# Regrouping a unit's sixteen products in an FFN up projection: by width, in place of alternating widths

## The chip, the cores and the metric

The kernel runs on one core of one Trainium2 chip. The metric is the device time of one execution in microseconds; the time before is the median of three runs.

## The reference, cut to what matters

One layer of a hybrid encoder trunk on 256 tokens of width 2048, in float32:

```python
h = rms_norm(x, attn_norm);  p = h @ w_in          # 2048 -> 5376 columns, then attention and a gated recurrence
x = x + concat(attn_out, hg_out) @ w_out           # 2048 -> 2048
h = rms_norm(x, ffn_norm)
u = h @ w_up                                       # 2048 -> 11264 columns, the projection that is changed
u = sum(conv_w[j] * up[:, j:j + S] for j in range(3)) + conv_b
a, b = split(u, 2)
x = x + (silu(a) * b) @ w_down                     # 5632 -> 2048
```

## The kernel before, in words

Precision is kept by splitting. Every float32 weight tile is split into a high part `w_hi` (ScalarE's copy to fp32r, `make_hi`, line 445) and a remainder `w_lo` (VectorE's subtraction, `make_lo`, line 781), and the activations lie in `hs` as high and low halves side by side: `hs[:, tile, 0:256]` is the high part of 256 tokens, `hs[:, tile, 256:512]` the low part. A product of two split numbers is three products: high x high, high x low and low x high.

Weights come in units of 128x1024 float32 (512 KB), through a ring of four slots (`RING = 4`) with one buffer each of `raw`, `w_hi` and `w_lo` per slot. For a slot the order is: SyncE's queue loads `raw` once VectorE has split what was in it before (semaphore `units_split`, lines 325 to 329); ScalarE makes `w_hi` once the load has landed and TensorE has used the unit before it in this slot (`loaded`, `units_used`, lines 442 to 445); VectorE makes `w_lo` (lines 779 to 782) and counts `units_split`; TensorE waits for that count, multiplies, and counts `units_used` with the unit's last product.

The up projection (`unit_channels`, line 1254) has 44 groups of 256 output channels, four units to a group, so 176 units. A unit is four tiles of the contraction (k) times two tiles of 128 output channels (b), and each of these eight has its own accumulator bank. Per k and b it issues two products, each with its own weight load:

- line 1262: weights `w_hi`, moving `hs` in its full 512 columns, which is high x high and high x low at once, into all 512 columns of the bank;
- line 1263: weights `w_lo`, moving the 256 columns of the high half, added into the first 256 columns of the same bank.

So before the change the widths go 512, 256, 512, 256 and so on, 16 products to a unit. When a group is done VectorE adds the two halves of each bank (`evacuate`, line 784) and runs two taps of the convolution (`taps`, line 1170); ScalarE runs the third tap and the silu. Two pairs of banks alternate between groups (`pair_of`, line 285). Lines 1544 to 1560 issue the stage: two groups written out, then a loop of 21 with two groups in each turn.

Two other helpers show what TensorE does with one width alone. `unit_w_in` (line 1267) issues 24 products of 256 columns, lines 1276, 1278 and 1279. `unit_tokens` (line 1283, output and down projections, lines 1292 to 1294) and `unit_i_and_g` (line 1419, lines 1428 to 1430) issue 12 products of 512 columns each. In all of them each product has a 128x128 weight load of its own, as here.

Of the kernel before, what the change touches and what calls it, by code (L numbers as in the profile page):

```python
# [38 lines left out]
P = 128  # L39
D_MODEL, SEQ, CHUNK = 2048, 256, 64  # L40
# [7 lines left out]
RING = 4  # L48
FREE = 1
BANK_PAIRS = 2  # L50
GC = 256
# [37 lines left out]
def hybrid_layer(nc, x, attn_norm, w_in, q_norm, k_norm, sinks, lb_logits, hg_norm, w_out,  # L89
                 ffn_norm, w_up, conv_w, conv_b, w_down, out):  # L90
    ctx = ExitStack()
    with ctx:
        def sb(name, shape, dt=F32):
            return ctx.enter_context(nc.sbuf_tensor(name, shape, dt))
# [13 lines left out]
        hs = sb("hs", [P, KT, 2 * SEQ], F32R)  # L108
        raw = sb("raw", [P, RING, 1024])
        w_hi = sb("w_hi", [P, RING, 1024], F32R)  # L110
        w_lo = sb("w_lo", [P, RING, 1024], F32R)
# [173 lines left out]
        def pair_of(group):  # L285

            b = 2 * ((group + 1) % BANK_PAIRS)
            return bank[b], bank[b + 1]
# [937 lines left out]
        def _(pe):  # L1226
            def transpose(dst, src, n=P):
                return pe.transpose(dst, src, ident[0:n, 0:n])  # L1228
# [25 lines left out]
            def unit_channels(quad, i, group):  # L1254

                pe.wait_ge(units_split, quad * RING + i + 1 + RING)
                banks = pair_of(group)
                for k in range(4):
                    for b in range(2):
                        c = slice(k * GC + b * P, k * GC + (b + 1) * P)  # L1260
                        x_k = hs[:, 4 * i + k, :]
                        pe.matmul(banks[b][:, :], w_hi[:, i, c], x_k, start=(i == 0 and k == 0), stop=False)  # L1262
                        last = pe.matmul(banks[b][:, 0:SEQ], w_lo[:, i, c], x_k[:, 0:SEQ], start=False,  # L1263
                                         stop=(i == RING - 1 and k == 3))
                last.then_inc(units_used, 1)

            def unit_w_in(quad, i, dst):
# [48 lines left out]
            for i in range(RING):  # L1316
                pe.wait_ge(h_lo, 2 * i + 2)
                unit_w_in(0, i, bank[0])
                if i == 2:
# [4 lines left out]
                    for c in range(1 + CONV):  # L1324
                        at = N_SMALL + c * N_CONV
                        last = transpose(bank[3][:, at:at + N_CONV], rows[0:N_CONV, 1 + c, :], N_CONV)
# [218 lines left out]
            for i in range(RING):  # L1545
                pe.wait_ge(h_lo, (CHUNKS + i + 1) * TT)
                unit_channels(Q_UP, i, G_UP)
                if i == 1:
                    second_norm(OUT_GROUPS - 1)
            pe.wait_ge(groups_evacuated, G_UP + 2)  # L1550
            for i in range(RING):
                unit_channels(Q_UP + 1, i, G_UP + 1)
                if i == 0:

                    spread_rms(1)
            with pe.Fori(1, UP_GROUPS) as g:
                for ab in range(2):
                    pe.wait_ge(groups_evacuated, g * 2 + ab + G_UP + 1)
                    for i in range(RING):
                        unit_channels(g * 2 + ab + Q_UP, i, G_UP + ab)  # L1560
# [37 lines left out]
```

## Time and profile before

| what | before |
|---|---|
| median of 3 runs | 1123.79 us (1123.77 to 1123.81) |
| the profiled execution, its own time | 1132.9 us |
| its span, first to last instruction | 1131.1 us |
| TensorE (matmul) busy | 1122.8 us, 99% |
| TensorE weight load busy | 972.9 us, 86% |
| VectorE busy | 786.8 us, 70% |
| ScalarE busy | 588.8 us, 52% |
| DMA | 204.26 MB, mean 181 GB/s |
| granted TensorE clock over the span | 0.999 |

All durations below come from the one profiled execution, which is 9.1 us longer than the median of the runs without a profile. In the timeline a row is one instruction: its start, its duration, the engine, the line of the kernel, what it writes and reads. Matmuls are pipelined: one starts while the one before it is still draining, so the duration in a row is longer than the step from one start to the next, and the pace of TensorE is read from the starts. The up projection's first product starts at 388.76 us and its last at 887.77 us of the span.

### The profile page before, as it was taken

How to read it: one execution, taken by the hardware profiler on the slowest of the kernel's cores; microseconds unless marked ns; L12 is line 12 of the kernel's file. 1: busy time of each engine (PE TensorE's matmuls, PEld its weight loads, DVE VectorE, ACT ScalarE, POOL GpSimd, SP SyncE). 2: the span in 40 equal slices, each digit the busy share in tenths (PEclk: the TensorE clock that was granted, in tenths of full speed). 3: DMA queues.
4: the chain of work that ended last, by engine and by line, in shares of the span. 5: the costliest groups of instructions: out<-in, count | busy, mean ns of one | idle time of the engine just before them, and what ended most of it. 6: DMA issues, size and time to landing. Idle time of an engine off the chain costs nothing.

```text
span 1131.1 us, 18722 instructions
## 1 busy us (share of the span) xinstructions
PE 1122.8 (99%) x6593; PEld 972.9 (86%) x6593; DVE 786.8 (70%) x1178; ACT 588.8 (52%) x863; POOL 11.1 (1%) x43
## 2 busy tenths in 40 slices
PE   9999999999999999999999999999999999999998
PEld 8989898989888888888888888888888888888887
DVE  5788968778755577777777777777777745454443
ACT  7678565657444565555555555555555533433332
POOL 3000000000000000000000000000000000000000
PEclk9999999999999999999999999999999999999999
DMA  8544555554556556555656565556665566666562
GB/s 264 154 148 120 179 154 166 164 172 150 171 184 188 186 175 193 184 186 185 186 184 187 184 187 185 186 184 187 185 186 183 188 192 195 210 194 211 191 214 80
DMA packets 172514, 204.26 MB, mean 181 GB/s; under 512 B 6949, under 2 KB 140470, under 8 KB 172214
## 3 DMA queue, kind: packets, MB, share of 16 engines
q1 hardware_dynamic: 171302, 201.55, 57.5%
q10 hardware_dynamic: 1168, 2.11, 0.5%
q8 instruction: 28, 0.46, 0.2%
q14 instruction: 16, 0.13, 0.0%
HBM read 201.54 MB, written 2.10 MB: 180 GB/s over the span
## 4 chain that ended last, share of the span: by engine, by line
PE 89%; DVE 7%; ACT 3%; issue 0%; ACTq 0%; DVEq 0%
PE bank L1262 29%; PE bank L1263 15%; PE bank L1292 10%; PE bank L1294 10%; PE bank L1293 10%; PE bank L1276 3%; PE bank L1278 3%; PE bank L1279 3%; DVE w_lo L781 2%; ACT w_hi L445 1%; PE bank L1228 1%; PE bank L1428 1%; DVE E L997 1%; DVE E L976 1%; PE bank L1429 1%; PE bank L1430 1%
## 5 line engine op out<-in xcount | busy, mean ns | idle before, releaser
L781 DVE TENSOR_TENSOR w_lo<-raw,w_hi 128x1024 fp32r<-128x1024 f32 x380 | 463.1, 1223 | 285.8 <-ACT w_hi L445 285.1
L445 ACT CAST w_hi<-raw 128x1024 fp32r<-128x1024 f32 x380 | 398.3, 1052 | 455.2 <-PE bank L1263 197.7
L1262 PE MATMUL bank<-hs,w_hi 128*128 128x512 f32 x1408 | 497.9, 399 | 0.2 <-DVE hs L801 0.2
L1263 PE MATMUL bank<-hs,w_lo 128*128 128x256 f32 x1408 | 395.4, 281 | 0.0
L1262 PEld LDWEIGHTS bank<-hs,w_hi 128*128 128x128 f32 x1408 | 264.6, 188 | 66.5 <-DVE hs L801 0.5
L1263 PEld LDWEIGHTS bank<-hs,w_lo 128*128 128x128 f32 x1408 | 265.9, 189 | 0.1
L1293 PE MATMUL bank<-w_lo,gated 128*128 128x512 f32 x352 | 136.9, 389 | 0.0
L1292 PE MATMUL bank<-w_hi,gated 128*128 128x512 f32 x352 | 136.9, 389 | 0.0
L1294 PE MATMUL bank<-w_hi,gated 128*128 128x512 f32 x352 | 136.9, 389 | 0.0
L1276 PE MATMUL bank<-hs,w_hi 128*128 128x256 f32 x416 | 120.5, 290 | 0.6 <-DVE w_lo L781 0.6
L1278 PE MATMUL bank<-hs,w_hi 128*128 128x256 f32 x416 | 117.6, 283 | 0.0
L1279 PE MATMUL bank<-hs,w_lo 128*128 128x256 f32 x416 | 117.6, 283 | 0.0
L1276 PEld LDWEIGHTS bank<-hs,w_hi 128*128 128x128 f32 x416 | 79.6, 191 | 3.0 <-issue 2.6
L1278 PEld LDWEIGHTS bank<-hs,w_hi 128*128 128x128 f32 x416 | 79.7, 192 | 0.4 <-issue 0.2
L1279 PEld LDWEIGHTS bank<-hs,w_lo 128*128 128x128 f32 x416 | 79.6, 191 | 0.0
L1294 PEld LDWEIGHTS bank<-w_hi,gated 128*128 128x128 f32 x352 | 66.1, 188 | 13.8
L1293 PEld LDWEIGHTS bank<-w_lo,gated 128*128 128x128 f32 x352 | 66.1, 188 | 13.7
L1292 PEld LDWEIGHTS bank<-w_hi,gated 128*128 128x128 f32 x352 | 66.1, 188 | 13.6
L1179 DVE SCALAR_TENSOR_TENSOR C<-U,cols,C 128x256 f32<-128x256 f32 x176 | 73.4, 480 | 0.0
L727 ACT ACTIVATE C<-U,cols 128x256 f32<-128x256 f32 x88 | 48.2, 595 | 25.3 <-DVE U L792 25.3
L1428 PE MATMUL bank<-w_hi,hs 128*128 128x512 f32 x128 | 50.8, 397 | 0.0
L1292 PE MATMUL bank<-w_hi,mix 128*128 128x512 f32 x128 | 50.3, 393 | 0.0
(189 smaller groups left out, 957.4 us busy)
## 6 DMA issues: line engine op xcount, KB each, us to landing
raw<-in_w_ffn_up_dram SPq DMA_DIRECT2D x176, 512.0 KB, 3.5
raw<-in_w_ffn_down_dram SPq DMA_DIRECT2D x88, 512.0 KB, 4.4
raw<-in_w_in_dram SPq DMA_DIRECT2D x52, 512.0 KB, 3.8
raw<-in_w_in_dram SPq DMA_DIRECT2D x64, 256.0 KB, 2.9
raw<-in_w_out_dram SPq DMA_DIRECT2D x32, 512.0 KB, 3.9
xt<-in_x_dram SPq DMA_DIRECT2D x2, 1024.0 KB, 6.0
out_dram<-xt ACTq DMA_DIRECT2D x3, 512.0 KB, 6.7
out_dram<-xt ACTq DMA_DIRECT2D x2, 256.0 KB, 2.5
```

Of the source, the lines that this page charges most:

```text
L445: act.copy(w_hi[:, i, :], raw[:, i, :]).then_inc(units_hi, 1)
L781: dve.tensor_tensor(w_lo[:, i, :], raw[:, i, :], w_hi[:, i, :].bitcast(F32), ALU.subtract)\
L1179: dve.scalar_tensor_tensor(C[:, ab, c, :], U[:, c, tap:tap + SEQ], cols[:, bass.ds(col, 1)], C[:, ab, c, :], ALU.mult, ALU.add).then_inc(a ...
L1262: pe.matmul(banks[b][:, :], w_hi[:, i, c], x_k, start=(i == 0 and k == 0), stop=False)
L1263: last = pe.matmul(banks[b][:, 0:SEQ], w_lo[:, i, c], x_k[:, 0:SEQ], start=False, stop=(i == RING - 1 and k == 3))
L1276: pe.matmul(o, w_hi[:, i, c], x_hi, start=(i == 0 and k == 0 and b == 0), stop=False, skip_group_check=True)
L1278: pe.matmul(o, w_hi[:, i, c], x_lo, start=False, stop=False, skip_group_check=True)
L1279: last = pe.matmul(o, w_lo[:, i, c], x_hi, start=False, stop=(i == RING - 1 and k == 3), skip_group_check=True)
L1292: pe.matmul(banks[t][:, :], x_hi, hi, start=(k0 + k == 0), stop=False)
L1293: pe.matmul(banks[t][:, :], x_hi, lo, start=False, stop=False)
L1294: last = pe.matmul(banks[t][:, :], x_lo, hi, start=False, stop=(k0 + k == k_all - 1))
L1428: pe.matmul(o, x_hi, hi, start=(u == 0 and k == 0), stop=False)
```

## The change

Within `unit_channels` the one loop over k and b becomes two. The first issues the eight 512-column products with `w_hi`, the second the eight 256-column products with `w_lo`. The same sixteen products with the same operands go into the same banks. Consecutive products now go to the two banks in turn, where before two in a row went to each. The wait at the start, the start flag on the first product of each bank, and the count `units_used` on the last product of the unit stay.

```diff
                 for k in range(4):
                     for b in range(2):
                         c = slice(k * GC + b * P, k * GC + (b + 1) * P)
-                        x_k = hs[:, 4 * i + k, :]
-                        pe.matmul(banks[b][:, :], w_hi[:, i, c], x_k, start=(i == 0 and k == 0), stop=False)
-                        last = pe.matmul(banks[b][:, 0:SEQ], w_lo[:, i, c], x_k[:, 0:SEQ], start=False,
-                                         stop=(i == RING - 1 and k == 3))
+                        pe.matmul(banks[b][:, :], w_hi[:, i, c], hs[:, 4 * i + k, :],
+                                  start=(i == 0 and k == 0), stop=False)
+                for k in range(4):
+                    for b in range(2):
+                        c = slice(k * GC + b * P, k * GC + (b + 1) * P)
+                        last = pe.matmul(banks[b][:, 0:SEQ], w_lo[:, i, c], hs[:, 4 * i + k, 0:SEQ],
+                                         start=False, stop=(i == RING - 1 and k == 3))
                 last.then_inc(units_used, 1)
```

## Rows read from the trace of the kernel before

**Rows 1.** The page: span, busy time of the engines, granted clock.

```profile
span 1131.1 us, 18722 instructions
...
PE 1122.8 (99%) x6593; PEld 972.9 (86%) x6593; DVE 786.8 (70%) x1178; ACT 588.8 (52%) x863; POOL 11.1 (1%) x43
...
PEclk9999999999999999999999999999999999999999
```

**Rows 2.** Windows of 500:600 (up) and 888:1000 (down); busy by engine, clock, DMA.

```profile
500.00:600.00 100.00, 100.00 (x568) 86.67 (x567) 76.84 (x105) 51.53 (x62) 0.00 (x0) 1.00 0.60 187
...
888.00:1000.00 112.00, 112.00 (x496) 92.75 (x495) 55.93 (x52) 44.92 (x45) 0.00 (x0) 1.00 0.63 198
```

**Rows 3.** Waits in 410:880, up projection: total us, times, longest us.

```profile
ACT w_hi L445 <- PE bank L1263: 193.0, 140, 1.8
DVE w_lo L781 <- ACT w_hi L445: 100.8, 83, 1.6
```

**Rows 4.** The page's costliest groups: busy us, mean ns, idle before.

```profile
L1262 PE MATMUL bank<-hs,w_hi 128*128 128x512 f32 x1408 | 497.9, 399 | 0.2 <-DVE hs L801 0.2
L1263 PE MATMUL bank<-hs,w_lo 128*128 128x256 f32 x1408 | 395.4, 281 | 0.0
```

**Rows 5.** Timeline of PE, up projection, widths in turn: start us, us, instruction.

```profile
599.91 0.40 PE L1262 MATMUL bank<-hs,w_hi 128*128 128x512 f32 x1
600.15 0.28 PE L1263 MATMUL bank<-hs,w_lo 128*128 128x256 f32 x1
...
605.21 0.40 PE L1262 MATMUL bank<-hs,w_hi 128*128 128x512 f32 x1
```

**Rows 6.** Timeline of PE, a long run of 512-column products.

```profile
121.87 0.39 PE L1428 MATMUL bank<-w_hi,hs 128*128 128x512 f32 x1
...
132.75 0.39 PE L1428 MATMUL bank<-w_hi,hs 128*128 128x512 f32 x1
```

**Rows 7.** Timeline of PE, 256-column products right after a 512-column run.

```profile
143.40 0.28 PE L1276 MATMUL bank<-hs,w_hi 128*128 128x256 f32 x1
...
143.75 0.28 PE L1276 MATMUL bank<-hs,w_hi 128*128 128x256 f32 x1
143.87 0.28 PE L1278 MATMUL bank<-hs,w_hi 128*128 128x256 f32 x1
...
146.15 0.28 PE L1279 MATMUL bank<-hs,w_lo 128*128 128x256 f32 x1
```

**Rows 8.** Timeline of PE, first and sixth 512-column product after 256-column ones, twice.

```profile
117.09 0.40 PE L1428 MATMUL bank<-w_hi,hs 128*128 128x512 f32 x1
...
118.25 0.39 PE L1430 MATMUL bank<-w_hi,hs 128*128 128x512 f32 x1
...
887.88 0.40 PE L1292 MATMUL bank<-w_hi,gated 128*128 128x512 f32 x1
...
889.04 0.39 PE L1294 MATMUL bank<-w_hi,gated 128*128 128x512 f32 x1
```

**Rows 9.** Timeline of PE, the first three products of the up projection.

```profile
388.76 0.39 PE L1262 MATMUL bank<-hs,w_hi 128*128 128x512 f32 x1
388.99 0.28 PE L1263 MATMUL bank<-hs,w_lo 128*128 128x256 f32 x1
389.10 0.40 PE L1262 MATMUL bank<-hs,w_hi 128*128 128x512 f32 x1
```

**Rows 10.** Timeline of PE, up projection between two interruptions, widths in turn.

```profile
399.24 0.40 PE L1262 MATMUL bank<-hs,w_hi 128*128 128x512 f32 x1
...
403.40 0.40 PE L1262 MATMUL bank<-hs,w_hi 128*128 128x512 f32 x1
```

**Rows 11.** Timeline of ACT and DVE: the split of one unit.

```profile
608.24 1.05 ACT L445 CAST w_hi<-raw 128x1024 fp32r<-128x1024 f32 x1 [1.78 <-PE bank L1263]
...
609.56 1.22 DVE L781 TENSOR_TENSOR w_lo<-raw,w_hi 128x1024 fp32r<-128x1024 f32 x1
```

**Rows 12.** The page's DMA issues: count, KB each, us from issue to landing.

```profile
raw<-in_w_ffn_up_dram SPq DMA_DIRECT2D x176, 512.0 KB, 3.5
```

## The prediction

> **What bounds the kernel now.** I read the page first. TensorE is busy for 1122.8 of 1131.1 us and its granted clock is at the full level in all 40 slices [rows 1]. That says that TensorE carries the span and that no clock is to be won, but not that it runs at its best pace, because a pipelined matmul counts as busy while it drains. The page's groups show how far this goes: the 1408 products of line 1262 and the 1408 of line 1263 sum to 497.9 + 395.4 = 893 us of duration [rows 4], in a stage that lasts 499 us (388.76 to 887.77). So these durations can't be added, and the pace must be taken from starts.
>
> Next the windows by stage. In the up projection TensorE is busy for all of the 100 us, VectorE for 76.84, ScalarE for 51.53, and the DMA engines move 187 GB/s [rows 2]. The waits of the stage have no row for TensorE at all: ScalarE waits for TensorE (193.0 us in 140 waits) and VectorE for ScalarE (100.8 us) [rows 3]. Everyone waits, directly or through another, for TensorE to free a slot. The stage takes as long as TensorE needs for its stream of products, so what a reordering of the stream is worth is a question of start-to-start steps alone.
>
> So I read the timeline for three kinds of stretch. **Widths in turn**, as now: line 1262 starts at 599.91 and, 15 pairs later, at 605.21 [rows 5], so a pair takes 5.30 / 15 = 353.3 ns. **512 columns alone**: 48 steps from 121.87 to 132.75 [rows 6], 226.7 ns each. **256 columns alone**: 19 steps from 143.87 to 146.15 [rows 7], 120.0 ns each. Apart, the two widths would cost 226.7 + 120.0 = 346.7 ns; in turn they cost 6.7 ns more. That surplus, in 1408 pairs, is what the regrouping can reach.
>
> **The change, part by part.**
>
> *The runs.* A unit now takes 8 x 353.3 = 2826.7 ns. Two runs of eight at their own steady steps would take 8 x 226.7 + 8 x 120.0 = 2773.3 ns, 53.3 ns less.
>
> *The changes of width that remain*, one each way per unit where there were eight each way. Both occur alone in the trace. Going from 256 to 512 columns, the first five steps together take 1.16 us, both at 117.09 and at 887.88 [rows 8]; five steady steps are 1.133 us. The entry into 512 columns costs 27 ns, spread over five products, and then the pace is steady. Three more such entries, near 168, 219 and 270 us, show the same 1.16. The one at 887.88 comes out of the present alternation, so a single 256-column product ahead is enough to set it off; a run of eight should pay it once, and its last three products are at 226.7. Going from 512 to 256 columns, the four steps from 143.40 to 143.87 take 0.47 us against 0.48 steady [rows 7]: a gain of up to 10 ns, of which I take 7. Net, 20 to 21 ns of the 53.3 are paid back.
>
> *Sum.* 1813.3 + 27.7 = 1841 ns for the eight wide ones, 960 - 6.5 = 953.5 for the narrow ones: 2794.5 ns per unit, 32.2 less than now. Times 176 units: 5.7 us. Bounds from both sides: if the entry cost nothing, 53.3 x 176 = 9.4 us; if the 53.3 stays whatever the order, 0. I take the middle value because it has rows of its own kind, five of them alike, while both ends need that these rows don't carry over.
>
> *What could differ from those rows.* In the 512-column rows the moving operand is a weight tile, here it is `hs`. The first product of the stage speaks to that: line 1262 at 388.76, after a settled run of 512s, is followed 0.23 us later, not 0.24 as in mid-stage [rows 9, 5]. So a wide product with `hs` moving is not slow in itself. The banks alternate with each product instead of every second. In the 512-column run the bank changes after every sixth product, and no step of rows 6 stands out by as much as 10 ns; for 256 columns a change of bank at each product is not shown by itself. I take 0 for it and keep it in the slow rival below.
>
> *What hides the rest.* The number of products, weight loads, waits and counts is unchanged. `units_used` still comes with the unit's last product, so ScalarE, VectorE and SyncE's queue see the same order with a period 32 ns shorter. Is there room? ScalarE's copy at 608.24 begins as TensorE frees the slot, and VectorE's part ends at 609.56 + 1.22 = 610.78 [rows 11]; TensorE wants that slot after three other units, at 608.24 + 3 x 2.83 = 616.7, so it is ready 5.9 us early. The raw tile behind it lands 3.5 us after issue [rows 12], with most of a ring's turn of 11 us to do so. VectorE's 76.84 us of 100 become about 77.7. The loads must rise from 187 to about 189 GB/s; the down projection already moves 198 with TensorE busy throughout [rows 2]. If this cover were gone, a late VectorE would show first, as a wait before line 1262. The down projection starts 5.7 us earlier and keeps its length.
>
> [...]
>
> **The rivals.**
>
> 1. *The order of widths is not the cause.* The surplus belongs to something that stays, such as the switch between `w_hi` and `w_lo` loads within a unit, or it comes back in the runs. For it: eight pairs in a row were never measured otherwise. Against it: the settling steps of rows 8 are tied to a change of width, and lines 1292 to 1294 also switch between `w_hi` and `w_lo`, at 226.7. Time: 1123.8.
> 2. *Width changes cost nothing in short runs.* The five slow steps would be a debt that only a long 256-column stretch builds up. Against it: the entry at 887.88 had a single narrow product ahead. Time: 1123.8 - 9.4 = 1114.4.
> 3. *The wide run never settles, and the kernel is slower.* Place: the eight wide products of each unit, whose banks now alternate at each one. If each took what it takes in alternation (0.24 us [rows 5], 236.7 ns averaged over three pairs), a unit would cost 8 x 236.7 + 953.5 = 2847 ns, 20 more than now: +3.6 us, 1127.4. It turns to a loss from (2826.7 - 953.5) / 8 = 234.2 ns per wide product. Against it: rows 8 settle within five.
> 4. *The alternation is better than profiled.* Between two interruptions the present order ran 12 pairs from 399.24 to 403.40 [rows 10], 346.7 ns a pair: there is a second beat without the surplus. After 404 us it never returns in the profile. If executions without a profile kept that beat, the new unit would be 21 ns worse and the time 1123.8 + 3.7 = 1127.5. For it: the profiled execution is 9.1 us above the median, near 53.3 x 176 = 9.4. Against it: three runs within 0.04 us of each other, and a recording that itself may account for the difference. On that the Trainium skill, Runtime: NRT & Kernel Launch, gives a kernel-invariant 6.2 us; no run here shows it.
>
> **How the numbers follow.** The sum is made against the profiled execution, 1132.9 - 5.7 = 1127.2 us; I carry the same 5.7 to the median: 1123.79 - 5.67 = 1118.1. Chances: forecast 0.73, rival 1 0.10, rival 2 0.08, rival 3 0.04, rival 4 0.05. Forecast and rival 2 hold 0.81, so the range runs from rival 2's 1114.4 to 1122.0, where an entry cost of nearly twice the measured one (27 + 22 ns) would put it. A measurement can tell some 0.2%, 2.2 us, from no change: faster 0.81, same 0.10, slower 0.09.
>
> **What would show it.** In the profile of the changed kernel, six or more steps in a unit's wide run at 0.23, the first five summing to 1.16 us; narrow steps of 0.12 with the first at 0.11; a unit from first line 1262 to the next unit's first in 2.79 to 2.80 us, against 2.83; a stage of about 493 us; no wait of TensorE on line 781. A unit of 2.77 would be rival 2, of 2.83 rival 1, of 2.85 rival 3; 2.79 with an unchanged or longer median would be rival 4. A wait before a unit's first product would mean that my account of the cover is wrong.

## The result and the profile after

| | before | after |
|---|---|---|
| median of 7 runs each | 1123.81 us | 1127.41 us |
| lowest to highest | 1123.77 to 1123.95 | 1127.10 to 1128.72 |
| profiled execution, its own time | 1132.9 us | 1127.16 us |
| span of the profiled execution | 1131.1 us | 1125.4 us |

The change makes the kernel slower by 0.3%: the ratio of the times is 1.0033, interval 1.0021 to 1.0045. The forecast was 1118.1 us, so the sign is wrong. A few executions of nearly every kernel show a granted clock of 0.998 over the span and are some 1.4 us longer, here the one of 1128.72 us. But the two profiles differ by 5.7 us in the direction of the forecast and by its size. Both facts need the same explanation.

The page of the changed kernel, first its head, answering to [rows 1], and then the groups that answer to [rows 4]:

```profile
span 1125.4 us, 18722 instructions
...
PE 1116.7 (99%) x6593; PEld 973.8 (87%) x6593; DVE 786.9 (70%) x1178; ACT 589.2 (52%) x863; POOL 11.1 (1%) x43
...
PEclk9999999999999999999999999999999999999999
...
L1261 PE MATMUL bank<-hs,w_hi 128*128 128x512 f32 x1408 | 352.9, 392 | 0.2 <-DVE hs L801 0.2
...
L1266 PE MATMUL bank<-hs,w_lo 128*128 128x256 f32 x1408 | 196.3, 282 | 0.0
```

TensorE's busy time fell by 6.1 us and that of every other engine stayed within 1 us. The groups' busy sums fell from 893 to 549 us while the stage got shorter by about 6 us only: where products of one line overlap, the time is counted once, and where products of two lines overlap, it is counted in both groups. That is why these sums were not used.

The waits of 410:880 and the windows, answering to [rows 3] and [rows 2]:

```profile
ACT w_hi L445 <- PE bank L1266: 185.6, 126, 1.8
DVE w_lo L781 <- ACT w_hi L445: 95.3, 83, 1.6
```

```profile
500.00:600.00 100.00, 100.00 (x575) 88.03 (x574) 78.65 (x108) 52.08 (x62) 0.00 (x0) 1.00 0.61 188
888.00:1000.00 112.00, 112.00 (x496) 92.78 (x495) 53.92 (x49) 43.98 (x43) 0.00 (x0) 1.00 0.63 197
```

TensorE again has no row among the waits, and its windows hold 575 products in place of 568 per 100 us. The timeline of TensorE, where a row now holds a run of eight (start, duration, instruction, count):

```profile
600.02 2.00 PE L1261 MATMUL bank<-hs,w_hi 128*128 128x512 f32 x8
601.87 1.11 PE L1266 MATMUL bank<-hs,w_lo 128*128 128x256 f32 x8
602.82 2.00 PE L1261 MATMUL bank<-hs,w_hi 128*128 128x512 f32 x8
...
627.96 0.40 PE L1261 MATMUL bank<-hs,w_hi 128*128 128x512 f32 x1
```

Ten units from 600.02 to 627.96 are 2.794 us each. The wide run takes 1.85 us (steady steps would be 1.813), the narrow one 0.95. The forecast had 2794.5, 1841 and 953.5 ns. So within the profiles each step came out as worked out, and what failed was to take the profile of before for what the kernel does in its timed runs.

### The profile page after: what moved, and what is told of

Its sections match the earlier page's. It is cut to its first block, busy times and chain, and to the rows that moved or that the text cites. A ratio compares the mean times of both kernels' runs of the same rounds, so it can differ in the third digit from the quotient of the medians.

```text
span 1125.4 us, 18722 instructions
## 1 busy us (share of the span) xinstructions
PE 1116.7 (99%) x6593; PEld 973.8 (87%) x6593; DVE 786.9 (70%) x1178; ACT 589.2 (52%) x863; POOL 11.1 (1%) x43
## 4 chain that ended last, share of the span: by engine, by line
PE 89%; DVE 7%; ACT 3%; DMA 1%; issue 0%; SPq 0%; ACTq 0%; DVEq 0%
PE bank L1261 29%; PE bank L1266 15%; PE bank L1297 10%; PE bank L1295 10%; PE bank L1296 10%; PE bank L1279 3%; PE bank L1282 3%; PE bank L1281 3%; DVE w_lo L781 2%; ACT w_hi L445 1%; PE bank L1228 1%; PE bank L1431 1%; DVE E L976 1%; DVE E L997 1%; PE bank L1432 1%; PE bank L1433 1%
## 5 line engine op out<-in xcount | busy, mean ns | idle before, releaser
L1261 PE MATMUL bank<-hs,w_hi 128*128 128x512 f32 x1408 | 352.9, 392 | 0.2 <-DVE hs L801 0.2
L1261 PEld LDWEIGHTS bank<-hs,w_hi 128*128 128x128 f32 x1408 | 253.3, 189 | 45.8 <-DVE hs L801 0.4
L1266 PEld LDWEIGHTS bank<-hs,w_lo 128*128 128x128 f32 x1408 | 192.1, 190 | 13.7
L1266 PE MATMUL bank<-hs,w_lo 128*128 128x256 f32 x1408 | 196.3, 282 | 0.0
L1282 PE MATMUL bank<-hs,w_lo 128*128 128x256 f32 x416 | 117.6, 283 | 0.0
L1279 PEld LDWEIGHTS bank<-hs,w_hi 128*128 128x128 f32 x416 | 79.6, 191 | 3.0 <-issue 2.6
L1281 PEld LDWEIGHTS bank<-hs,w_hi 128*128 128x128 f32 x416 | 79.7, 192 | 0.4 <-issue 0.2
L1282 PEld LDWEIGHTS bank<-hs,w_lo 128*128 128x128 f32 x416 | 79.6, 191 | 0.0
```

The source lines that it names most:

```text
L1261: pe.matmul(banks[b][:, :], w_hi[:, i, c], hs[:, 4 * i + k, :], start=(i == 0 and k == 0), stop=False)
L1266: last = pe.matmul(banks[b][:, 0:SEQ], w_lo[:, i, c], hs[:, 4 * i + k, 0:SEQ], start=False, stop=(i == RING - 1 and k == 3))
L1279: pe.matmul(o, w_hi[:, i, c], x_hi, start=(i == 0 and k == 0 and b == 0), stop=False, skip_group_check=True)
L1281: pe.matmul(o, w_hi[:, i, c], x_lo, start=False, stop=False, skip_group_check=True)
L1282: last = pe.matmul(o, w_lo[:, i, c], x_hi, start=False, stop=(i == RING - 1 and k == 3), skip_group_check=True)
```

## The experiments

All regroup the products of `unit_channels`, or what stands around it. Time is the median of the executions of that label; beside each ran the kernel before on the same chip.

### e1: the kernel before, profiled again

No edit.

> The kernel before, unchanged, profiled and timed again. Theory (two beats): widths in turn have two steady beats, 353.3 ns a pair (the profile read before the prediction) and 346.7 ns (seen there only from 399 to 404 us); ordinary executions run on the fast one. Then all times are near 1123.8, and a profile taken of such an execution has a span near 1122.0, an up stage of about 490 us and pairs of 346.7 ns. Rival (the recording): a profile always slows this order by about 9 us and not the regrouped one. Then the span is again near 1131 with pairs of 353.3 ns while the times are 1123.8.

Measured: 1123.86 us, ten executions from 1123.79 to 1125.47 and one at 1132.86. The profiled one took 1124.0. From the new profile the head of its page; then, from the view of line 1262 alone, the wide products with their first and last start; then its window of 500:600, as in [rows 2]; then two rows of its timeline, 15 pairs apart as in [rows 5]:

```profile
span 1122.2 us, 18722 instructions
```

```profile
L1262 PE MATMUL bank<-hs,w_hi x1408: 389/395/577, 389.0 to 878.6; 128*128 128x512 f32 x176
```

```profile
500.00:600.00 100.00, 100.00 (x579) 87.46 (x578) 79.16 (x108) 52.43 (x63) 0.00 (x0) 1.00 0.61 189
```

```profile
599.90 0.40 PE L1262 MATMUL bank<-hs,w_hi 128*128 128x512 f32 x1
...
605.11 0.39 PE L1262 MATMUL bank<-hs,w_hi 128*128 128x512 f32 x1
```

5.21 us in 15 pairs is 347 ns, not 353.3. Over the whole loop it is finer: the first unit starts at 413.06 us and the 168th at 876.20, so a unit takes 463.14 / 167 = 2773.3 ns and a pair 346.7. The wide products run from 389.0 to 878.6, where in the profile read before the prediction they ran from 388.8 to 887.5. That is 9.1 us, and it is all of the difference between 1131.1 and 1122.2 within 0.2. The same program has two steady beats (a beat is a pace that a repeating sequence of steps holds), and a recording costs nothing that shows here: the profiled execution (1124.0) stands beside the others (1123.86). The theory of the two beats holds, the rival falls. Over all comparisons the kernel before was timed 94 times, and 7 executions were above 1130 us: 3 of them in the comparison of e9 and e10, where all three of its executions were. The other experiments ran on other chips, and whether the chip has a part in it is not settled.

From here on the unit of 2773.3 ns, eight times 226.7 + 120.0, is the floor to which orders are compared.

### e2 and e3: shorter runs

```diff
                 for k in range(4):
                     for b in range(2):
...
                         pe.matmul(banks[b][:, :], w_hi[:, i, c], hs[:, 4 * i + k, :],
                                   start=(i == 0 and k == 0), stop=False)
-                for k in range(4):
                     for b in range(2):
...
                         last = pe.matmul(banks[b][:, 0:SEQ], w_lo[:, i, c], hs[:, 4 * i + k, 0:SEQ],
```

That is e2, against the regrouped kernel, so that the second loop over b lies within the first loop over k; e3 does the same with k in two halves of two, so that runs are four long.

> Per k two wide products, then two narrow ones (512, 512, 256, 256). Theory (each entry into a wide run pays again): wide steps of 234 and 235.5 ns, narrow ones of 114 and 119.5, 703 ns for two pairs, a unit of 2812 ns, 39 above the fast beat's 2773; 1123.8 + 6.8 = 1130.6 us. Rival (a short run finds a beat without surplus, as the alternation does): 2773 ns a unit and 1123.8 us.

> Four wide, four narrow, twice in a unit. Theory (each entry pays): 234 + 235.5 + 228.5 + 232 = 930 ns and 114 + 119.5 + 120 + 120 = 473.5 ns, a unit of 2807 ns, 1123.8 + 6.0 = 1129.8 us. Rival (the cost is one per unit, whatever the number of runs): as the regrouped kernel, 1127.4. Rival (short runs find a fast beat): 1123.8.

Measured: e2 1126.03 us (one of its ten executions took 2924.55 us, which nothing here explains), e3 1129.42 us. From the timelines, e2 and then e3:

```profile
600.21 0.63 PE L1261 MATMUL bank<-hs,w_hi 128*128 128x512 f32 x2
...
602.99 0.40 PE L1261 MATMUL bank<-hs,w_hi 128*128 128x512 f32 x1
```

```profile
600.88 1.09 PE L1262 MATMUL bank<-hs,w_hi 128*128 128x512 f32 x4
601.81 0.63 PE L1267 MATMUL bank<-hs,w_lo 128*128 128x256 f32 x4
602.28 1.09 PE L1262 MATMUL bank<-hs,w_hi 128*128 128x512 f32 x4
...
603.69 1.09 PE L1262 MATMUL bank<-hs,w_hi 128*128 128x512 f32 x4
```

Runs of four cost what the sum of settling steps gives: 2.81 us for a unit (603.69 - 600.88), 2807 expected, and 1129.4 for 1129.8. Runs of two don't: 2.78 us for a unit (602.99 - 600.21) and, by the time, (1126.0 - 1123.8) / 176 = 13 ns above the floor, where the theory said 39 and the rival 0. A run too short to settle can end in a cheaper pattern than the sum of first steps. So the surplus doesn't simply grow with the number of changes of width: runs of one 0 or 53 ns per unit, of two 13, of four 33, of eight 20.

### e4: the banks

```diff
-                for k in range(4):
-                    for b in range(2):
+                for b in range(2):
+                    for k in range(4):
```

in both loops of the regrouped kernel.

> Eight wide and eight narrow as in the regrouped kernel, but four to one bank and then four to the other. Theory (only the widths matter): the regrouped kernel's time, 1127.4 us, and the same five slow steps after each entry. Rival (the change of bank at each product costs): near 1123.8, with the entry's five slow steps gone.

Measured: 1127.22 us. Its timeline:

```profile
601.50 2.00 PE L1261 MATMUL bank<-hs,w_hi 128*128 128x512 f32 x8
603.34 1.12 PE L1266 MATMUL bank<-hs,w_lo 128*128 128x256 f32 x8
604.29 2.00 PE L1261 MATMUL bank<-hs,w_hi 128*128 128x512 f32 x8
```

A unit of 2.79 and a wide run of 1.84 us, as with the banks in turn. The order of the banks is worth nothing that shows: 1127.22 us against 1127.41.

### e7: runs of sixteen

```diff
-                        unit_channels(g * 2 + ab + Q_UP, i, G_UP + ab)
+                        unit_channels(g * 2 + ab + Q_UP, i, G_UP + ab, "narrow first" if i % 2 else "wide first")
```

and the same for the two groups ahead of the loop, with a further argument of `unit_channels` for the order of its products, so that one unit's narrow run goes on in the next one's.

> Units alternate between wide first and narrow first, so that runs are sixteen long and there is one entry into a wide run per two units. Theory (each entry into a wide run costs about 27.6 ns and each way back gives 6.5 to 7): 2773.3 + 20.6 / 2 = 2783.7 ns a unit, 1123.8 + 1.8 = 1125.6 us. Rival (the regrouped order costs by its narrow or wide products as such): as the regrouped kernel, 1127.4.

Measured: 1125.59 us. Its timeline:

```profile
601.78 3.82 PE L1270 MATMUL bank<-hs,w_hi 128*128 128x512 f32 x16
605.44 2.08 PE L1273 MATMUL bank<-hs,w_lo 128*128 128x256 f32 x16
607.35 3.82 PE L1270 MATMUL bank<-hs,w_hi 128*128 128x512 f32 x16
```

5.57 us for two units, 2785 each, 2783.7 expected. Half the entries, half the surplus: this gives the entry's price (20 ns net per entry and way back, 3.5 us over 176 units) by itself, and with e3 says where the regrouped kernel's 3.6 us over the ordinary kernel before are.

### e5, e6, e11 and e12: what sets the beat

With the same further argument, in e5 and e6 all units stay in turn but one, the last ahead of the loop:

```diff
-                unit_channels(Q_UP + 1, i, G_UP + 1)
+                unit_channels(Q_UP + 1, i, G_UP + 1, "narrow first" if i == RING - 1 else "in turn")
```

(e6: wide first). In e11 all units are as before, and in e12 the unit of e5 stays; both put this behind that unit, ahead of the loop:

```diff
+            for n in range(8):
+                transpose(bank[4 + n // 4][:, (n % 4) * P:(n % 4 + 1) * P], ident[:, :])
             with pe.Fori(1, UP_GROUPS) as g:
```

> The order in turn everywhere, but one unit, the last ahead of the loop, issues its eight narrow products first and its eight wide ones then, so that the loop's alternation is entered from a settled wide run. In both profiles of the kernel before, an entry from a settled wide run (at 388 us) leads into the beat with the surplus. Theory (the way in sets the beat): the loop runs at 2827 ns a unit, and the time is near 1132.8 us in all executions. Rival (the beat is drawn at random, or the fast one is the rule): 1123.8 us as before.

> The same with that one unit wide first, narrow after, so that the alternation is entered from a settled narrow run. Theory (the way in sets the beat) doesn't say which of the two beats this entry gives, but every execution should give the same one: 1123.8 or 1132.8 us, with no scatter between executions. Rival (random): mostly 1123.8, now and then 1132.8.

> The kernel before with eight 128-column transposes of a constant (their result is not used) ahead of the loop, so that the alternation is entered anew from them. In the profiles of the kernel before, the alternation is on the fast beat after the eight transposes at 396 us, whatever it was on ahead of them. Theory (the way in sets the beat): the fast beat in every execution, 1123.8 plus about 1.0 for the transposes, 1124.8 us, with none near 1133, also where executions of the kernel before beside it are. Rival (something else sets it): scatter as in the kernel before, with some near 1134.

> The kernel of e5 (one unit narrow first, wide after, which gave the beat with the surplus in all ten executions) with the same eight transposes behind that unit. Theory (the last way in counts): the fast beat again, near 1124.8 us. Rival (the unit regrouped once, or the shift in time that it brings, sets the beat by something other than the way in): 1133.8 us.

Measured:

| | median us | executions | lowest to highest |
|---|---|---|---|
| e5, one unit narrow first | 1132.92 | 10 | 1132.69 to 1134.32 |
| e6, one unit wide first | 1132.86 | 10 | 1132.71 to 1134.48 |
| e11, break ahead of the loop | 1124.78 | 11 | 1124.62 to 1126.29 |
| e12, the unit of e5, then the break | 1124.96 | 10 | 1124.68 to 1126.30 |

Sixteen products in another order near 410 us, out of 2816, cost 9 us over the 470 us that follow. e5's timeline, 15 pairs apart, and then e12's:

```profile
599.80 0.40 PE L1270 MATMUL bank<-hs,w_hi 128*128 128x512 f32 x1
...
605.10 0.40 PE L1270 MATMUL bank<-hs,w_hi 128*128 128x512 f32 x1
```

```profile
599.63 0.39 PE L1270 MATMUL bank<-hs,w_hi 128*128 128x512 f32 x1
...
604.83 0.39 PE L1270 MATMUL bank<-hs,w_hi 128*128 128x512 f32 x1
```

5.30 us against 5.20: the slow beat and the fast one. e5 and e12 differ by eight transposes only, and all ten executions of the one are slow, all ten of the other fast. So the way in sets the beat, and in e5's profile it then holds through all 168 units of the loop. e11 by itself says less: none of its 11 executions was on the slow beat, but neither was any of the 21 of the kernel before beside it, so that the transposes fend off the slow beat in the plain kernel is likely by e12, not shown.

Where does the plain kernel choose? The last interruption ahead of the loop is at line 1331 (a small product that spreads a row of norms), and behind it the two profiles are on different beats. First the profile of before, then e1:

```profile
404.09 0.59 PE L1331 MATMUL bank<-rms_diag,all_mean 128*128 128x256 f32 x2
...
404.87 0.40 PE L1262 MATMUL bank<-hs,w_hi 128*128 128x512 f32 x1
...
405.93 0.40 PE L1262 MATMUL bank<-hs,w_hi 128*128 128x512 f32 x1
```

```profile
404.30 0.59 PE L1331 MATMUL bank<-rms_diag,all_mean 128*128 128x256 f32 x2
...
405.08 0.40 PE L1262 MATMUL bank<-hs,w_hi 128*128 128x512 f32 x1
...
406.12 0.39 PE L1262 MATMUL bank<-hs,w_hi 128*128 128x512 f32 x1
```

Three pairs take 1.06 us in the one and 1.04 in the other, and so it stays to the end of the stage. But the two part earlier. From the stage's start their steps agree within 1 ns up to some 398.5 us, where TensorE has waited for VectorE's `hs` (line 801). The four steps from there are 341, 118, 231 and 113 ns in the profile of before and 336, 117, 235 and 117 in e1. Both go on at 346.7 ns a pair, in different sequences, and only line 1331 brings one of them onto the slow beat. In e11's profile, where the products up to here are the same, this wait leads onto the slow beat: its 12 pairs in the stretch of [rows 10] take 4.24 us, not 4.16.

```profile
399.19 0.40 PE L1262 MATMUL bank<-hs,w_hi 128*128 128x512 f32 x1
...
403.43 0.40 PE L1262 MATMUL bank<-hs,w_hi 128*128 128x512 f32 x1
```

Behind line 1331 it is on the fast beat, before it comes to the added transposes. So an interruption can change the beat either way, the last one ahead of the loop decides, and differences of a few nanoseconds in how the products restart go with it. What makes those nanoseconds isn't settled.

### e8, e9 and e10: is it the narrow product's weight load?

```diff
-                        last = pe.matmul(banks[b][:, 0:SEQ], w_lo[:, i, c], hs[:, 4 * i + k, 0:SEQ],
+                        last = pe.matmul(banks[b][:, 0:SEQ + P], w_lo[:, i, c], hs[:, 4 * i + k, 0:SEQ + P],
```

in the regrouped kernel (e8) and in turn (e9); e10 is e8 with the wide products cut to the same 384 columns.

> The regrouped order with the narrow products 384 columns wide instead of 256 (they add low x low for 128 tokens). Theory (a 256-column step of 120 ns is set by the next weight load, and what the entry costs is that state being worked off): a 384-column step is 384 x 226.7 / 512 = 170 ns, longer than a load, so the first wide steps are 226.7 ns at once, a unit is 8 x 226.7 + 8 x 170 = 3173 ns, and the time is 1123.8 + 70.4 = 1194.2 us. Rival (any change of width costs): five slow steps stay, 3194 ns a unit, 1197.9 us.

> Widths in turn, 512 and 384 columns. The steady steps, if each product takes its columns at 2.4 GHz plus 13.3 ns as 512 alone (226.7) and 256 alone (120.0) do, are 226.7 + 173.3 = 400 ns a pair, 3200 ns a unit, 1123.8 + 75.1 = 1198.9 us. Theory (a product next to one of another width costs more, whatever the width): above that, and, with eight times as many neighbours of another width as the regrouped 512 and 384, not below its 3267 ns a unit and 1210 us. Rival (beats: alternation can lock into a cheap pattern that long runs can't): below 1210, down to 1198.9.

> All sixteen products of a unit 384 columns wide, in the regrouped order, the same 6144 columns a unit as in the kernel before. The wide products leave out high x low for 128 of the tokens. Theory (no change of width within the stage, so no surplus): sixteen steps of 173.3 ns, 2773 ns a unit, near 1123.8 us and no second beat. Rival (384 columns are irregular by themselves, which would also explain the regrouped 512 and 384): steps scattered from 173 to 185 ns, a unit of 2830 ns or more, 1134 us.

Measured: e8 1210.03 us, e9 1216.90, e10 1123.72. From the timelines of e8 and of e10:

```profile
602.41 2.01 PE L1261 MATMUL bank<-hs,w_hi 128*128 128x512 f32 x8
604.26 1.58 PE L1266 MATMUL bank<-hs,w_lo 128*128 128x384 f32 x8
605.68 1.55 PE L1261 MATMUL bank<-hs,w_hi 128*128 128x512 f32 x6
```

```profile
601.35 1.55 PE L1261 MATMUL bank<-hs,w_hi 128*128 128x384 f32 x8
...
604.12 1.55 PE L1261 MATMUL bank<-hs,w_hi 128*128 128x384 f32 x8
```

In e10 sixteen products take 2.77 us (604.12 - 601.35), 173 ns each: 384 columns by themselves are as regular as 256 and 512, and all three widths fit columns / 2.4 GHz plus 13.3 ns. My 170 ns for e8 was too low for that. By 173.3 its unit would be 3200 ns; it takes 3.27 us, with a wide run of 1.85 and a narrow one of 1.42 (1.813 and 1.387 steady), so more is lost at 384 than at 256. The load theory fell: a product longer than its neighbour's load loses more, not less. In turn (e9) it is worst: eight pairs take 3.31 us, 3307 ns a unit over the loop, where the steady steps add up to 3200.

```profile
599.91 0.40 PE L1262 MATMUL bank<-hs,w_hi 128*128 128x512 f32 x1
...
603.22 0.40 PE L1262 MATMUL bank<-hs,w_hi 128*128 128x512 f32 x1
```

No beat without surplus was seen in its two executions. The rival of e10 fell too. What is left is the statement that the runs support: products of one width follow each other at a regular step, and products of different widths don't, except on the fast beat of 512 and 256 in turn, which costs no more than the steady steps. Why the chip does so stays open.

Beside e9 and e10 the kernel before ran at 1132.9 to 1134.5 us in all three executions, so their ratios to it (1.0732 and 0.991) are not used; their times are compared with 1123.8.

## Why the prediction was wrong

- **What bounds the kernel, the cover, the order of banks, the other engines**: right, by the waits after and by e4.
- **The pace of the present order, 353.3 ns a pair**: right for the profile, wrong for the kernel. This is the step that failed. In nearly all timed executions a pair takes 346.7 ns and a unit 2773 ns (e1's profile, and 87 of 94 times). That the one profile read fell on the rarer beat was chance; that its time was 9.1 us off the median was there to be seen.
- **The settling cost, 27.7 ns on the way in and 6.5 back**: right. 2794 ns were measured for 2794.5, and e7 halved it.
- **"I carry the same 5.7 to the median"**: wrong, from 1132.9 to a median of 1123.79. The regrouped order shows one beat only, in its profile and in its seven times; 20 ns more than 2773 in 176 units are 3.5 us, 3.6 measured.
- **Rival 4**, with 0.05, is what happened, at 1127.5 for 1127.41. Its mechanism, [rows 10] and the near match of 9.1 and 9.4 us were all in the text. Two arguments put it down. Three runs within 0.04 us of each other speak only against a beat drawn anew each time; a beat that nearly always comes out the same leaves no scatter either, and 87 of 94 executions were below 1130. And the difference was ascribed in part to the recording. The Trainium skill, Runtime: NRT & Kernel Launch, section "The ~15µs preamble/postamble breakdown", gives some 6.2 us between a profile's total time and the time that the runtime reports. That is a gap between two measures of one execution, and no run here shows it; 1132.9 and 1123.79 are the same measure of two executions. In e1 the profiled execution lies 0.1 us from the median, and its own time is 1.8 us above its span.
- **Rivals 1 to 3** fell by the profile after, with its unit of 2.794 us. The order of widths does matter: the regrouped unit takes 20 ns more than the fast beat and 33 less than the slow one.

## What to carry to other kernels

Compare the profiled execution's own time with the median before working out a sum, and when they differ by as much as the gain in question, look in the profile for the same code at two paces: the stretch at the better one may be what the timed runs do. An order of matmuls of mixed widths has a steady pace of its own that needn't be the sum of the widths' own steps; take it from starts, over a stretch that repeats, and expect that a small change ahead of a long loop can move it by 2%. With all products of one width (e10) the pace was regular, and both executions took the same time.

## What the runs showed of the hardware that was not expected

- One program, two steady beats: 346.7 or 353.3 ns for a 512- and a 256-column product in turn, at a granted clock of 1.00 in both, held for 470 us. The choice was made by the few products ahead: 20 of 20 executions slow behind one regrouped unit, 10 of 10 fast when eight transposes followed it. In the plain kernel two profiles whose steps had agreed within 1 ns parted by 5 ns behind a wait, and ended on different beats.
- The step of a product among its like is columns / 2.4 GHz plus 13.3 ns: 120.0, 173.3 and 226.7 ns at 256, 384 and 512 columns.
- The first five 512-column products behind a 256-column one take 27 ns more together, whether they follow one narrow product ([rows 8]), eight (after) or sixteen (e7). Behind 384-column products (e8) they had not settled after eight: the last three steps of a run were 236, 229 and 232 ns.
